# Loading norm vectors and gate bias as rows, with three reorderings, in an eight-core encoder layer

## What is computed

```python
h = rmsnorm(x, norm1_g)                      # mean square over 1024 channels, f32
z = h @ w_in                                 # 1024 -> 1536: pool channels a | u | v
u, v = gelu(u), gelu(v)
# mixer A: trailing means over 2/4/8/16 tokens minus the token, a 128x128 map per group, a scale
# mixer B: per head of 128 channels and chunk of 128 tokens
mixed = einsum('gij,bnjgd->bnigd', masked(gmlp_ws), v) + gmlp_b   # masked: block-causal, 64 wide
gmlp_out = u * mixed
x = x + concat(pool_out, gmlp_out) @ w_out
x = x + square(relu(rmsnorm(x, norm2_g) @ w_up)) @ w_down         # 1024 -> 4096 -> 1024
y = rmsnorm(x, normf_g)
```

## Time and profile before

| | us |
|---|---|
| median of 3 runs | 1230.1 |
| lowest and highest | 1226.98, 1233.09 |
| the profiled execution | 1228.81 |
| its span, first to last instruction, slowest core (core 7) | 1227.2 |
| busy in that span: TensorE, VectorE, ACT, GpSimd | 1176.3, 803.3, 439.0, 154.3 |

### The profile page before, as it was taken

The page is one execution under the profiler, slowest core; times in us unless marked ns, Lnnn a source line. Parts: engine busy times, 40 slices in busy tenths (PEclk is TensorE's granted clock), DMA queues, the critical chain, the costliest instruction groups (busy, mean ns, idle before and its releaser), DMA issues.

```text
span 1227.2 us, 21475 instructions; the slowest of 8 cores (1212.3 to 1227.2 us)
## 1 busy us (share of the span) xinstructions
PE 1176.3 (96%) x7412; PEld 699.8 (57%) x7412; DVE 803.3 (65%) x1163; ACT 439.0 (36%) x678; POOL 154.3 (13%) x303
## 2 busy tenths in 40 slices
PE   5889999999899999999999999999999999899995
PEld 2547446544444587447754686447754686446842
DVE  3564546475668676857687676957687676766673
ACT  3346022323410464135521464035521464033401
POOL 3011000202200320022000210022001210021001
PEclk7899999999899999999999999999999999899998
DMA  9996898989996896769866895679765996769993
GB/s 197 170 211 171 207 241 217 214 323 307 310 323 240 262 318 211 261 229 321 287 219 227 280 331 217 236 246 314 271 234 207 308 332 145 238 224 307 310 318 134
DMA packets 65819, 310.41 MB, mean 253 GB/s; under 512 B 10784, under 2 KB 10848, under 8 KB 44976
## 3 DMA queue, kind: packets, MB, share of 16 engines
q1 hardware_dynamic: 49904, 239.35, 59.1%
q0 software_dynamic: 15664, 69.15, 21.8%
q10 hardware_dynamic: 144, 0.52, 0.1%
HBM read 277.90 MB, written 53.31 MB: 270 GB/s over the span
## 4 chain that ended last, share of the span: by engine, by line
PE 87%; DMA 7%; DVE 3%; issue 2%; ACT 1%; POOL 0%; DVEq 0%; SPq 0%; POOLq 0%; ACTq 0%
PE ps L755 26%; PE ps L666 22%; PE ps L536 9%; PE ps L421 9%; PE ps L592 6%; PE ps L578 5%; PE ps L442 4%; PE ps L617 3%; PE ps L375 2%; DMA RING<-scr_um 2%; DMA WV<-gmlp_ws 2%; DMA XS<-xall 1%; DMA scr_um<-RING 1%; DMA RING<-scr_up 1%; DVE PQ L476 1%
## 5 line engine op out<-in xcount | busy, mean ns | idle before, releaser
L755 PE MATMUL ps<-RING,ST 128*128 128x512 bf16 x1120 | 259.2, 381 | 0.3 <-DVE ST L728 0.3
L352 ACT ACTIVATE JUNK<-XS 128x1024 uint8<-128x1024 f32 (+1 forms) x100 | 105.6, 1056 | 326.4 <-DVE XS L541 235.2
L755 PEld LDWEIGHTS ps<-RING,ST 128*128 128x128 bf16 x1120 | 109.3, 98 | 128.2 <-issue 4.7
L666 PE MATMUL ps<-H2T,RING 128*128 128x256 bf16 x1536 | 178.9, 272 | 2.4 <-DVE ST L695 1.2
L666 PEld LDWEIGHTS ps<-H2T,RING 128*128 128x128 bf16 x1536 | 148.9, 98 | 31.4 <-issue 6.6
L765 DVE TENSOR_TENSOR XS<-XS,ps 128x512 f32<-128x512 f32 x140 | 95.8, 685 | 74.6 <-PE ps L755 70.3
L666 PE MATMUL ps<-SB,RING 128*128 128x256 bf16 x1152 | 138.8, 272 | 1.6 <-DMA RING<-scr_um 1.3
L359 POOL TENSOR_SCALAR SM<-SM 128x1 f32<-128x1 f32 (+2 forms) x96 | 33.1, 344 | 760.9 <-ACT JUNK L352 759.8
L666 PEld LDWEIGHTS ps<-SB,RING 128*128 128x128 bf16 x1152 | 111.2, 98 | 17.9 <-issue 3.0
L421 PE MATMUL ps<-HT,WAU 128*128 128x512 bf16 (+2 forms) x512 | 118.5, 380 | 1.4 <-ACT HT L379 1.4
L717 ACT ACTIVATE ST<-ST 128x1024 bf16<-128x1024 bf16 x96 | 101.4, 1057 | 38.6 <-DVE ST L707 34.2
(11 more groups left out here) (105 smaller groups left out, 1359.4 us busy)
## 6 DMA issues: line engine op xcount, KB each, us to landing
RING<-scr_dn SPq DMA_DIRECT2D x98, 1024.0 KB, 6.2
RING<-scr_um SPq DMA_DIRECT2D x120, 512.0 KB, 9.2
RING<-scr_up SPq DMA_DIRECT2D x48, 512.0 KB, 9.5
RING<-w_mlp POOLq DMA_DIRECT2D x16, 1024.0 KB, 14.3
yall<-XS POOLq DMA_DIRECT2D x29, 512.0 KB, 8.8
RING<-scr_wo SPq DMA_DIRECT2D x14, 1024.0 KB, 5.9
XS<-xall POOLq DMA_DIRECT2D x24, 512.0 KB, 11.9
scr_up<-RING POOLq DMA_DIRECT2D x8, 1024.0 KB, 13.7
```

Source lines behind the costliest of these rows:

```text
L352: add("act", lambda e: e.activation(out=JUNK[0:np_], in_=ap, func=AF.Square, scale=1.0 / 32, accum_out=SS[kind][0:np_, j:j + 1]), reads=re ...
L666: i_ = e.matmul(bank(ub)[:, u * 256:(u + 1) * 256], lhsT=RING[s][:, h * 4 + k, c0 + u * 128:c0 + (u + 1) * 128], rhs=op[:, k, :], start=(f ...
L755: i_ = e.matmul(bank(ub)[:, :], lhsT=lh(kk), rhs=RING[s][:, kk, :], start=(c == 0 and kk == 0 and M not in CONT), stop=(c == 1 and kk == 7 ...
```

## The change

Four edits. The norm 1 vector is loaded as one row of 4 KB into partition 0 of x slot 5, the gate bias and the norm 2 vector as rows into slots 7 and 6, at the same places of the same issuers' lists. A new helper `spread` multiplies a column of ones with 512 values of such a row on TensorE in f32, which gives the row on all 128 partitions of a PSUM bank, and VectorE copies that to `G1B`, `G2B` or `BB`. For norm 1 this stands between 8 and 10 spare matmuls in place of the 24; for norm 2 and the bias it stands ahead of the transposes of the third x tile. The fourth and fifth weight sums of a pass move by one step forward and two back. In c = 1 the N2 scalings and transposes of group 2 move one step forward, so that all four scalings come ahead of the first sum. For the last group the v product of the sample tile moves from step 19 to step 15, with the mask behind it, and the first `WI_au` from 15 to 16.

```diff
@@ -191,6 +191,7 @@
         PWF = GFB[:, 0:512].rearrange("p (g c) -> p g c", c=128)
         PWT = GFB[:, 512:768].bitcast(BF16).rearrange("p (g c) -> p g c", c=128)
         INVC = GFB[:, 768:832]
+        ONES = GFB[0:1, 896:1024]
         WSMTS = WV[:, 0, :].rearrange("p (g c) -> p g c", c=128)
         ZR = MIXP[:, 0, :]
         PSC = GFB[:, 832:836]
@@ -561,6 +562,12 @@
                     return i_
                 add("pe", mm, reads=[("MIXP", 0)], writes=[("BANK", fb)])
 
+            def spread(x, c0, out, res):
+                fb = next_front()
+                add("pe", lambda e: e.matmul(bank(fb)[:, :], lhsT=ONES, rhs=XS[0:1, x, c0:c0 + 512], start=True, stop=True),
+                    reads=["ONES", ("X", x)], writes=[("BANK", fb)])
+                add("dve", lambda e: e.tensor_copy(out=out, in_=bank(fb)[:, :]), writes=[("BANK", fb), res])
+
             HID = (lambda j, t0, t1: STF[:, j * 384 + t0:j * 384 + t1], lambda j, t0, t1: STF[:, 6144 + j * 256 + t0:6144 + j * 256 + t1])
 
             def hid_res(h, j):
@@ -787,9 +794,10 @@
 
             add("dve", lambda e: e.memset(ZR, 0.0), writes=[("MIXP", 0)])
             add("dve", lambda e: e.memset(MHALF, -0.5), writes=["MHALF"])
+            add("dve", lambda e: e.memset(ONES, 1.0), writes=["ONES"])
             add("dve", lambda e: e.memset(WSMT[64:128, :, 0:64], 0.0), writes=["WSMTz"])
             add("dve", lambda e: e.memset(A[:], 0.0), writes=[("A", g) for g in range(4)] + [("Ah", g) for g in range(4)])
-            add("act", lambda e: e.dma_start(out=G1B[:], in_=g1.partition_broadcast(128)), writes=["G1B"], dma="su1")
+            add("act", lambda e: e.dma_start(out=XS[0:1, 5, :], in_=g1.rearrange("(p c) -> p c", p=1)), writes=[("X", 5)], dma="su1")
             add("sp", lambda e: e.dma_start(out=XH, in_=xh[:, :]), writes=[("X", 9)], dma="su2")
             for n in range(3):
                 load_x(0, n, "sp")
@@ -804,11 +812,13 @@
                     reads=[("X", 2)], writes=[xres(1, n)], dma=f"xldsp{slot_x(1, n)}")
             add("sp", lambda e: e.dma_start(out=PSC, in_=pool_scale[:, :]), writes=["PSC"], dma="su5")
             add("sp", lambda e: e.dma_start(out=PWF, in_=pool_wt[:, :, :]), writes=["GFB"], dma="su7")
-            add("sp", lambda e: e.dma_start(out=BB[:].rearrange("p g c -> p (g c)"),
-                                            in_=gmlp_b.rearrange("g c -> (g c)").partition_broadcast(128)),
-                writes=["BB"], dma="sb0")
-            add("sp", lambda e: e.dma_start(out=G2B[:], in_=g2.partition_broadcast(128)), writes=["G2B"], dma="su3")
-            spare(24)
+            add("sp", lambda e: e.dma_start(out=XS[0:1, 7, 0:512], in_=gmlp_b.rearrange("(p g) c -> p (g c)", p=1)),
+                writes=[("X", 7)], dma="sb0")
+            add("sp", lambda e: e.dma_start(out=XS[0:1, 6, :], in_=g2.rearrange("(p c) -> p c", p=1)), writes=[("X", 6)], dma="su3")
+            spare(8)
+            spread(5, 0, G1B[:, 0:512], "G1B")
+            spread(5, 512, G1B[:, 512:1024], "G1B")
+            spare(10)
 
             sq("1", 3, XH, [("X", 9)], 16)
             rs("1", 3, 4, 16)
@@ -825,6 +835,9 @@
                 rs("1", n, n + 1)
                 N1_apply(0, n)
                 N1_T(0, n - 1)
+            spread(6, 0, G2B[:, 0:512], "G2B")
+            spread(6, 512, G2B[:, 512:1024], "G2B")
+            spread(7, 0, BB[:].rearrange("p g c -> p (g c)"), "BB")
             N1_T(0, 2)
             for j in range(2):
                 add("pool", lambda e, j=j: e.dma_start(out=WV[:, 4 * j:4 * j + 4], in_=w_v[:, 4 * j:4 * j + 4]),
@@ -873,7 +886,7 @@
             for n in range(4):
                 load_x(2, n, "sp")
             add("sp", lambda e: e.dma_start(out=GFB[:], in_=gf.partition_broadcast(128)),
-                writes=["GFB", "INVC", "PSC"] + [("PWT", g) for g in range(4)], dma="su4")
+                writes=["GFB", "INVC", "PSC", "ONES"] + [("PWT", g) for g in range(4)], dma="su4")
             for n in range(3):
                 for hh in range(2):
                     WO(0, n, hh)
@@ -929,7 +942,7 @@
                             main.append(L(pair_DN, q, hh, j0, h, n))
                 q11, q21, q12, q22 = 8 + c, 10 + c, 12 + c, 14 + c
                 u = lambda k: nup + k
-                ws = dict(w=(5, 6, 10, 12, 14))
+                ws = dict(w=(5, 6, 10, 11, 16))
                 side(u(ws["w"][0]), L(wsum, 6, c, q11, q12, ALU.add, 0))
                 side(u(ws["w"][1]), L(wsum, 7, c, q21, q22, ALU.add, 1))
                 side(u(ws["w"][2]), L(wsum, 1, c, q11, q22, ALU.add, 0))
@@ -951,7 +964,7 @@
                     for n in range(2):
                         side(u(e0["v"][n]), L(WI_v, 2, n))
                 else:
-                    e1 = dict(v=(1, 3), pl=(0, 1, 2, 3), gt=(8, 8, 9, 10), wo=(14, 15, 16, 17, 18, 19, 20, 21), nq=(21, 22, 23, 24), rs=(23, 23, 25, 25), na=(2, 3, 4, 5), nt=(5, 6, 8, 9), fq=(16, 17, 18), fo=(19, 19, 19))
+                    e1 = dict(v=(1, 3), pl=(0, 1, 2, 3), gt=(8, 8, 9, 10), wo=(14, 15, 16, 17, 18, 19, 20, 21), nq=(21, 22, 23, 24), rs=(23, 23, 25, 25), na=(1, 2, 3, 4), nt=(4, 5, 7, 8), fq=(16, 17, 18), fo=(19, 19, 19))
                     for n in range(2):
                         side(e1["v"][n], L(WI_v, 2, 2 + n))
                     for g in range(4):
@@ -1004,6 +1017,8 @@
                     tn = dict(sq=(15, 17, 19, 21), ap=(18, 20, 22, 24), tr=(23, 27, 27, 30), v=(36, 37, 39, 39), au=(31, 31, 33, 34, 35, 36, 37, 38), pl=(34, 36, 38, 39))
                 else:
                     tn = dict(sq=(2, 5, 7, 11), ap=(3, 6, 9, 12), tr=(5, 8, 11, 14), v=(6, 11, 14, 19), au=(15, 16, 18, 18, 20, 21, 23, 24), pl=(18, 18, 21, 22), fq=(0, 0), fo=(1, 7), lx=(2, 4))
+                    if j == LAST:
+                        tn.update(v=(6, 11, 14, 15), au=(16, 16, 18, 18, 20, 21, 23, 24))
                     for n in (2, 3):
                         side(tn["fq"][n - 2], L(final_sq, i - 1, n), L(final_rs, n, n + 1))
                         side(tn["fo"][n - 2], L(final_out, i - 1, n))
```

## The result

The changed kernel takes **1246.3 us** (median of four runs, 1244.7 to 1248.1). Against the kernel before on the same chip the ratio is **1.0136, 95% interval 1.0117 to 1.0154**: some 17 us slower. The forecast was 1242 us, slower; direction and mechanism held, the size came out larger, and two steps of the sum were wrong: the clock of the first projection, and the fifth weight sum, which had been counted at nothing. In some executions the cores of a die run at a lower granted clock and take some per cent longer (1346.7 us in one of the kernel before); ratios and means over runs leave these out.

The account below looks back on a forecast made before the run. TensorE was taken as the bound. On core 0, forecast the slowest, 1226.5 + 15.5 (setup) - 1.5 (scalings) - 0.3 (mask) = 1240.2 us, with 1.6 us around it 1242 us; range 1226 to 1248.

Parts of the forecast that it names:

- The rows' landing: Setup, SP's queue: norm 2 and gate bias rows land at 34.0 us, bounds 29.3 and 37.
- The products: Setup, TensorE: each f32 product for norm 2 and bias takes 1.7 us, 5.1 for three; bounds 0.46 and 3.0.
- The products for norm 1: Setup: two f32 products and copies hidden by the third x tile, counted at nothing; some 5 us without that cover.
- The clock: First projection: products ahead of it win back 2.95 us of half clock, so it takes 10.7 us, not 13.66.
- The delay travels on: After the setup: the first projection ends 15.5 us later, and this delay reaches the later stages.
- Rival 1: Later TensorE finds weights there already, so waits for transfers shrink and the delay is given back: 1233 us, chance 0.12.
- Scalings: c = 1: N2 scalings ahead of the waiting weight sum end the stage 1.8 us earlier, 1.5 on core 0.
- The fifth sum: c = 0: moving it from step 14 to 16 delays its store, counted at nothing, at most +2 us.
- The mask: Last group's gate: the earlier sample mask removes TensorE's wait, -5.95 us on core 7, -0.3 on core 0.
- The sum: Whole kernel: terms added per core, core 7 to 1234.9 us and core 0 to 1240.2 us.
- Core 0, forecast as the slowest: Whole kernel: core 0 becomes the slowest, going from 1226.5 to 1240.2 us.

Follow-up runs that it names:

- rows_act_late: Changed kernel with the norm 2 and gate bias rows issued as late as before, but on ACT's queue: 1236.5 us, in one run.
- front_only: Kernel before with rows for broadcasts, all at the head of ACT's queue, and all five products ahead of the first x tile's transposes: ratio 1.0018.
- prod_moved: Changed kernel with only the three products for norm 2 and gate bias moved behind the first projection in TensorE's order: 1227.6 us, ratio 0.9989.
- warm72: Changed kernel with 72 more spare matmuls of zeros ahead of the three late products: 1248.3 us, ratio 1.0141.
- rows_only: Changed kernel with weight sums, N2 scalings and sample mask as in the kernel before, leaving only rows and products: 1251.0 us, ratio 1.0164.
- mask_only: Kernel before with only the sample mask moved forward: 1228.6 us, ratio 0.9980.
- rows_early: Changed kernel with the norm 2 and gate bias rows issued on ACT's queue right behind the norm 1 row: 1231.3 us, ratio 1.0010.

## Why the prediction was right or wrong

**The rows' landing** was right: 34.0 forecast, 34.10 on core 7, 32.6 to 35.8 over the cores, from what the small transfers behind the x tiles had shown. That it hit to 0.1 us is luck. The forecast went by the landing of the pool weights, and that came at 14.38 + 20.8 = 35.2 us, 1.0 earlier than before and not 2.7, with the row 1.1 ahead of it and not 0.5 behind:

```profile
14.38 0.44 SPq L814 DMA_DIRECT2D GFB<-pool_wt  x1
...
GFB<-pool_wt SPq DMA_DIRECT2D x1, 256.0 KB, 20.8
```

That an earlier issue buys little, as core 6 had suggested, does not hold across the cores: the four that issued the row at 12.2 to 12.6 us had it at 32.6 to 33.5, the four that issued it at 14.9 to 16.0 at 34.1 to 35.8. The Trainium skill's 2 us plus bytes (page "DMA: Bandwidth & Descriptors", section "Anatomy of one DMA"), which would have had the rows there by 19 us, differs from the measured landing by 15; that section is about DMAs that GpSimd issues, and SP issued these. By rows_act_late some 12 us go with what stands ahead in the same queue.

**The products** were right in size, 1.7 against 1.82 us, at half clock; the reason given ("several passes") can be made exact: the ten spare matmuls of front_only took 0.445 us each at that clock, and four of these are 1.78. The Trainium skill, page "FP8 and Floating Point Precision", section "TensorE Precision Notes", has true f32 as four passes, and the trace agrees. With this the bounds of 0.46 and 3.0 us would have been needless. (The 0.46 us of the earlier trace rows is the mean length of records that overlap; the 24 matmuls together took 6.9 us there.) The products for norm 1, counted at nothing, were covered in the changed kernel only because the late rows held everything up longer: in prod_moved the projection starts some 3.5 us later on the four cores where TensorE was at half clock behind them. That the products kept it there was not tried by itself.

**The clock** was the first step that failed. "It gets something back ... and now the products run ahead of it" took 10.7 us for the projection; it took 13.40, as before 13.66. Products at half clock did not raise it: in front_only on core 7 five of them took 8.9 us without a break, and the ten spare matmuls behind them still ran at half clock. warm72 shows that even 17.7 us of matmuls ahead of the products don't leave the projection at full clock. The projection's end came 18.6 us later on core 7, not 15.5; 16.9 us of it were left at "pair" (18.9 on the mean of the cores).

**The delay travels on**: right, 19.6 us at "pair" and 18.5 at the end in rows_only. Rival 1, a delay given back at the loads, accounts for at most about 2 us at c = 1 (rows_only, "pair" to "down"), and over all its runs the ends are 20.0 us later, so nothing was given back in the end.

**Scalings**: forecast -1.8 us on core 7 and -1.5 on core 0; they gain about 1.4 on the mean of the cores. **The fifth sum** was the second step that failed: "the store is held up by earlier ones anyway ... so I count nothing". It is the store that the sixth load waits for; the line that says so stood in the earlier trace rows, and the full price had been named (two steps, up to 6.9 us) and then dropped. It measured 4.5 us at the load, some 3.4 us at c = 1 on the mean of the cores where the scalings are forward, and 0.35% of the time alone. The layout of the stage itself was nearly right: on core 7 of the changed kernel "up" comes 21.8 us after the first sum's start (21.3 laid out, 23.0 before); what came out wrong is that this sum's weight was 3.4 us later than the setup's shift. Together the edit was to give 1.8 us and costs 1.8 in the changed kernel ("pair" to "down"), 3.5 when alone.

**The mask** was right: -5.70 us forecast as -5.95 on core 7, and on core 0 -0.3 ("fifth" to "sixth").

**The sum** for core 7 was +7.7 and is +15.5. The miss by steps, in its own milestones: setup 1.4, c = 1 3.9, the stages from "up" to "fifth" 3.5 that no step had, mask 0.3, and -1.4 behind it. The 3.5 us are no effect that can be told on one core: mask_only, which edits nothing between "up" and "fifth", moves by 5.1 us there on core 7. On the mean of the cores the stretch moves by 1.2.

Core 0, forecast as the slowest at +13.7, came out at +11.2. The slowest was core 5, and core 1, at +28.6, came within 2 us. Core 1 had no wait for the mask, or for the scalings at c = 1, in the profiled run of the kernel before, but that is no property of the core: it ended at 1212.3 us there and at 1221.3 on the mean of 78 runs, and it waits 5.1 us for the scalings in rows_only. Summing each core's own waits of one execution was therefore the wrong account, and that core 0's sum came near the measured time is in part luck. The mean of the eight cores is the steadier one: +17.4 us over all runs, and the slowest, whichever it is, went the same way (1.36%, 16.7 us).

## What to carry to other kernels

In this kernel a small transfer was about as late as the bytes queued ahead of it, and a product that waited for it held everything that stands behind it in its engine's order. Moving the transfer to an idle queue, or the product behind the next long block, took the loss away (rows_early, prod_moved). When a step is delayed, look which load is released by its store before counting it free. And when cores run the same program, don't add up the waits that one execution shows on one core, since another run has them on other cores: add up the mean of the cores, and let the slowest be a draw some us behind it.

## What the runs showed of the hardware that was not expected

- In much the same traffic, half a microsecond apart in issue, a 4 KB row took 6.5 us on ACT's idle queue and 18.8 us behind two x tiles and the pool weights on SP's (5.9 to 7.4 and 18.8 to 21.0 over the cores).
- The granted clock fell to half at 36 us in warm72 on core 7 although TensorE had worked nearly without a break since 15 us: from 33.65 to 36 us it ran f32 products of one row, after a wait of 0.92 us. In front_only on core 1 it fell without any wait: TensorE ran the five products back to back from 5.4 us, at 1.00 from 5 to 9 us, 0.55 from 9 to 11 and 0.50 from 11 to 15, where the ten spare matmuls start 0.43 us apart.
- Ahead of a core's first change of clock the column reads 1.00 whatever it is: in front_only on core 7 it is 1.00 from 5.3 to 19 us, where a spare matmul took 0.445 us; in rows_early ten of them took 2.33 us, 0.233 each. In that stretch the durations tell the clock, the column does not.
- With two one-row f32 products among the spare matmuls at the start, the cores part: at half clock through the ten matmuls behind them on four of eight in the changed kernel, at full clock on the others, with the transposes of the 16 tokens ahead at 13.3 to 13.5 us in place of 9.7 to 10.1.
